# Experts ranked by token count and written out as eight fixed widths in a decoder step

## The chip, the cores and the metric

The kernel runs on one core of a Trainium2 chip. The metric is the device time of one execution in microseconds (us); of several runs the median is given. Engines: PE multiplies matrices, VectorE (DVE), ScalarE (ACT) and GpSimd (POOL) do the elementwise work, SyncE (SP) issues most of the transfers.

## What is computed

One inference step of a two-layer decoder on 520 tokens (a prompt of 512 and 8 samples of one token), width 1024. Each layer has four token mixers behind one input and one output projection; then layer 0 has a dense SwiGLU, layer 1 a SwiGLU of eight experts of which each token takes two. All arithmetic is fp32. What matters here is the second:

```
logits = h @ w_router + b_router
top_v, top_i = top_k(logits, 2);  gates = softmax(top_v)
for e in range(8):
    y = y + comb[..., e:e+1] * ((silu(h @ w1[e]) * (h @ w3[e])) @ w2[e])
```

with h of 520 x 1024, w1[e] and w3[e] of 1024 x 1408, w2[e] of 1408 x 1024. There are 1040 (token, expert) pairs; each expert is computed only for its own.

## The kernel before, in words

The program is one function, `trunk_program`, with one block of code per engine; engines meet by semaphores. Adaptive norm weights, the mixers and the dense layer come first, in straight code (their products are in `product`, L747). Then comes layer 1's expert stage, the part that is changed.

**Routing** (DVE L1603 to L1644). From the router's logits DVE takes the two best experts of each token, counts tokens per expert (`countf`, `count`), sums them up in order of expert to each expert's first row (`ebase`, `first`), and computes each pair's row (`place`). ACT has turned h into rows meanwhile. POOL (L690 to L696) scatters the rows to a table in DRAM, h_by_expert, so that an expert's tokens are next to each other: 10 indirect transfers, 4 KB a row.

**The expert loop.** Every engine runs its own loop over the eight experts (`Fori(0, NE)`) and reads the expert's token count from SBUF into a register. Up to 256 tokens it takes the narrow path, above it a wide path for all 520 columns, which these inputs do not use. On the narrow path of PE:

- `narrow_rows` (L981): waits for the expert's rows, which SP has read into `stage` as two tiles of 128 rows (`first_rows`, L474), and transposes both to columns, 8 transposes a tile (L988). DVE (L1660) and ACT (L1308) copy them from PSUM to `hn`.
- `narrow_by_width` (L1071): a chain of If and Else over ten widths, from 128 to 256 columns; the first that holds the expert's tokens runs, each with its own copy of the code of `narrow_products` (L991).
- `narrow_products`: 11 blocks of w1 and w3 (L1006, 16 matmuls each), then 8 blocks of w2 (L1019, 11 matmuls each); ACT applies silu, DVE multiplies, and ACT copies the result to `yn`. An fp32 matmul shows in the trace as two MATMUL records, so an expert has 352 + 176. After each block of w2, `yn` of the block before is transposed back to rows (L1028, two tiles); DVE copies these to `yrow` (L1671). The last block's transposes wait for ACT's copy.

An expert's weights are 12 chunks (eight of w1 and w3 in turn, four of w2) in a ring of six slots. **SP's order** is written out by hand: the first six chunks of expert 0 when layer 1's projection is done (L464 to L466), then the wait for the scatter (`Rout`, L511), the row tiles of expert 0, and then, for each expert: the next expert's rows once this one's are transposed; each chunk's slot refilled when its products are done (L521 to L527); the expert's result written to y_by_expert (`rows_out`, L491). SP too branches on the count and loops.

**After the loop** POOL waits for the last of those writes (L698) and gathers each token's two results (L703); gating, residual and final norm follow in five tiles of rows, and the output is written.

Of the kernel before, what the change touches and what calls it, by code (L numbers as in the profile page):

```python
# [52 lines left out]
WIDTHS = [128, 136, 144, 152, 160, 176, 192, 208, 224, NW]  # L53
# [46 lines left out]
def trunk_program(nc, A, O):  # L100
    ctx = ExitStack()
    with ctx:
# [87 lines left out]
        ebase = sb("ebase", [P, NE])  # L190
        valid = sb("valid", [P, NT])
# [4 lines left out]
        countf = sb("countf", [P, NE])  # L196
        count = sb("count", [P, NE], I32)
        first = sb("first", [P, NE], I32)
# [98 lines left out]
        def norm_step(tag, k, n):  # L297
# [8 lines left out]
                                          "ya", "ss", "ssr", "rr", "scaled", "mods", "const"]}  # L306
# [16 lines left out]
        def tokens_of(eng, e):  # L323

            return eng.value_load(count[0:1, bass.ds(e, 1)], min_val=0, max_val=T)

        def first_of(eng, e):

            return eng.value_load(first[0:1, bass.ds(e, 1)], min_val=0, max_val=PICKS)
# [8 lines left out]
        def expert_chunk(e, j):  # L338

            if j < 8:  # L340
                w = A["w1_moe" if j % 2 == 0 else "w3_moe"][0]
                n = P * min(3, ET - 3 * (j // 2))
                return w[e].rearrange("(k p) n -> p k n", p=P)[:, :, (j // 2) * 384:(j // 2) * 384 + n], KD, n
            return A["w2_moe"][0][e].rearrange("(k p) n -> p k n", p=P)[:, :, (j - 8) * 256:(j - 7) * 256], ET, 256
# [47 lines left out]
        def _(sp):  # L392
# [71 lines left out]
            sp.wait_ge(*step(1, "po_done", KD))  # L464
            for j in range(EXPERT_RING):
                eload(j, expert_chunk(0, j))  # L466

            def used(e, j):

                if j < 8:  # L470
                    return R["f_done"], ET * e + min(3 * (j // 2) + 3, ET)
                return R["y_done"], KD * e + 2 * (j - 8) + 2

            def first_rows(row):  # L474

                for t in range(2):
                    sp.dma_start(stage[:, t, :], Hd[bass.ds(row + P * t, P), :]).then_inc(Rin[t], 16)

            def rest_of_rows(e):
                c, row = tokens_of(sp, e), first_of(sp, e)  # L480
                with sp.If(c <= NW):
                    for t in range(2, NT):
                        sp.sem_inc(Rwide[t - 2], 16)
                with sp.Else():
                    for t in range(2, NT):
                        free = sp.snap(sp.to_reg(NT * e + t - 1))
                        sp.wait_ge(const_ready, 1)
                        sp.wait_ge(R["in_tr"], free)
                        sp.dma_start(stage[:, t % 2, :], Hd[bass.ds(row + AT[t], P), :]).then_inc(Rwide[t - 2], 16)

            def rows_out(e):  # L491


                c, row = tokens_of(sp, e), first_of(sp, e)
                with sp.If(c <= NW):
                    sp.sem_inc(R["y_out"], 16 * (NT - 2))
                    for t in range(2):
                        there = sp.snap(sp.to_reg(NT * e + NT + t))
                        sp.wait_ge(const_ready, 1)
                        sp.wait_ge(R["yt_ev"], there)  # L500
                        sp.dma_start(Yd[bass.ds(row + P * t, P), :], yrow[:, t, :]).then_inc(R["y_out"], 16)
                with sp.Else():
                    for t in range(NT):
                        there = sp.snap(sp.to_reg(NT * e + t + 2))
                        sp.wait_ge(const_ready, 1)
                        sp.wait_ge(R["yt_ev"], there)
                        sp.dma_start(Yd[bass.ds(row + AT[t], P), :], stage[:, 2, :]).then_inc(R["y_out"], 16)

            sp.wait_ge(R["count"], 2)
            row0 = first_of(sp, 0)  # L510
# [3 lines left out]
            with sp.Fori(0, NE - 1) as e:  # L514
                rest_of_rows(e)
                row = first_of(sp, e + 1)
                free = sp.snap(sp.to_reg(NT * e + NT))
                sp.wait_ge(const_ready, 1)
                sp.wait_ge(R["in_tr"], free)
                first_rows(row)  # L520
                for j in range(PER_E):  # L521
                    which, n = used(e, j)
                    n = sp.snap(sp.to_reg(n))
                    sp.wait_ge(const_ready, 1)
                    sp.wait_ge(which, n)
                    j += EXPERT_RING
                    eload(j, expert_chunk(e, j) if j < PER_E else expert_chunk(e + 1, j - PER_E))  # L527
                rows_out(e)
            last = sp.snap(sp.to_reg(NE - 1))
            rest_of_rows(last)  # L530
            for j in range(PER_E - EXPERT_RING):
                sp.wait_ge(*used(NE - 1, j))
                eload(j + EXPERT_RING, expert_chunk(NE - 1, j + EXPERT_RING))
            rows_out(last)
# [18 lines left out]
        def _(pool):  # L553
# [23 lines left out]
            pool.memset(ebase[:], 0.0).then_inc(R["const"], 1)  # L577
# [120 lines left out]
            pool.wait_ge(R["y_out"], 16 * NE * NT + 16)  # L698
# [17 lines left out]
        def _(pe):  # L716
# [264 lines left out]
            def narrow_rows(e):  # L981

                pe.sem_inc(R["in_tr"], 1)
                for t in range(2):
                    pe.wait_ge(Rin[t], 16 * e + 16)
# [5 lines left out]
            def narrow_products(e, n):  # L991

                for f in range(ET):
                    c = f // 3
                    if f % 3 == 0:
                        chunk_here(e, 2 * c)
                        chunk_here(e, 2 * c + 1)
                    pe.wait_ge(R["f_free"], ET * e + f + 1)
                    m = P * min(3, ET - 3 * c)
                    for w in range(2):  # L1000
                        for k in range(KD):
                            if f == w == 0 and k == 0:
                                pe.wait_ge(R["in_ev"], NT * e + NT)
                            if f == w == 0 and k == 4:
                                pe.wait_ge(R["in_ev1"], 2 * e + 2)
# [3 lines left out]
                pe.wait_ge(R["yt_ev"], NT * e + 1)  # L1009
                pe.sem_inc(R["yt_tr"], 3)  # L1010
                for q in range(KD + 1):
                    if q < KD:
                        if q % 2 == 0:
                            chunk_here(e, 8 + q // 2)
                        pe.wait_ge(R["y_free"], KD * e + q + 1)
                        for k in range(ET):
                            if q == 0 and k in (0, ET - 1):
                                pe.wait_ge(R["f_free"], ET * e + (ET + 1 if k == 0 else ET + 2))
                            mm = pe.matmul(PP[2][:, q % 2, 0:n], expert_slot(8 + q // 2, ET, 256)[:, k, P * (q % 2):P * (q % 2) + P],  # L1019
                                           Gn[:, k, 0:n], start=(k == 0), stop=(k == ET - 1))  # L1020
                        mm.then_inc(R["y_done"], 1)
                    if q:
                        j = q - 1
                        pe.wait_ge(R["y_free"], KD * e + j + 3)
                        if j == 4:
                            pe.wait_ge(R["yt_ev"], NT * e + 4)
                        for t in range(2):
                            tr = pe.transpose(PP[3][:, t, (j % 4) * P:(j % 4) * P + P], yn[:, j, P * t:P * t + P], ident[:])  # L1028
                        if j % 4 == 3:
                            tr.then_inc(R["yt_tr"], 1)  # L1030
# [40 lines left out]
            def narrow_by_width(e, c, widths):  # L1071

                if len(widths) == 1:
                    narrow_products(e, widths[0])
                    return
                with pe.If(c <= widths[0]):
                    narrow_products(e, widths[0])
                with pe.Else():
                    narrow_by_width(e, c, widths[1:])

            pe.wait_ge(R["count"], 2)
            with pe.Fori(0, NE) as e:
                c = tokens_of(pe, e)
                with pe.If(c <= NW):
                    narrow_rows(e)
                    narrow_by_width(e, c, WIDTHS)
                with pe.Else():
                    wide(e)

            pe.wait_ge(R["f_free"], ET * NE + 2)  # L1090
# [8 lines left out]
            pe.wait_ge(R["y_free"], KD * NE + 2)  # L1099
            pe.wait_ge(R["yt_ev"], NT * NE + 1)  # L1100
# [636 lines left out]
```

## Time and profile before

| what | value |
|---|---|
| median of 3 runs | 1824.57 us (1823.91 to 1828.57) |
| span of the profiled execution | 1826.2 us |
| PE busy, share of the span | 1479.6 us, 81% |
| DVE, ACT, POOL busy | 602.4, 480.2, 397.8 us |
| chain that ended last | PE 66%, DVE 15%, issue 9%, DMA 5% |
| all transfers | 286.02 MB, mean 157 GB/s |

The span is what the profile shows of one execution, from its first to its last instruction; it is the profiled execution's own time, and no other is given for it. It lies 1.6 us above the median. "Busy" counts instructions in an engine, not waits; the chain is followed back from the last instruction, at each step to what released it, and "issue" in it is time in which an engine waited for nothing that the profile shows.

### The profile page before, as it was taken

What the parts mean: (1) busy time and instruction counts of PE and PEld (TensorE: products, weight loads), DVE (VectorE), ACT (ScalarE), POOL (GpSimd) and SP (SyncE); (2) the same over time, 40 slices, a digit from 0 to 9 for tenths busy, and PEclk for the clock granted to TensorE, in tenths of its full rate; (3) what the DMA queues carried; (4) which work ended last, traced back from release to release, by engine and by line L of the source; (5) the groups of instructions that cost most, each with busy time, mean ns of one, the idle gap of its engine ahead of it and who ended that gap; (6) DMA issues with size and microseconds to landing.
All of it is one profiled execution on the core that took longest, in us unless ns stands there. A gap on an engine that the chain in (4) does not pass through costs nothing.

```text
span 1826.2 us, 27269 instructions
## 1 busy us (share of the span) xinstructions
PE 1479.6 (81%) x11320; PEld 1411.8 (77%) x11321; DVE 602.4 (33%) x815; ACT 480.2 (26%) x662; POOL 397.8 (22%) x288
## 2 busy tenths in 40 slices
PE   5776877789999999989588859879796919949792
PEld 4555876679999999979577649869796919949692
DVE  6667697623112011146965320101101000000115
ACT  6677312422221122223133221111111100011114
POOL 1102560534434343434524020000000000000004
PEclk9998898899999999989899979889898959979896
DMA  9999121024333322322210469686685833637554
GB/s 321 300 337 316 48 91 46 28 70 120 93 87 98 105 93 56 96 93 70 69 47 6 164 218 306 209 295 210 241 269 183 300 109 110 216 104 234 173 171 163
DMA packets 249862, 286.02 MB, mean 157 GB/s; under 512 B 7589, under 2 KB 241719, under 8 KB 249686
## 3 DMA queue, kind: packets, MB, share of 16 engines
q1 hardware_dynamic: 244886, 272.17, 45.9%
q0 software_dynamic: 3632, 11.08, 1.8%
q8 instruction: 126, 2.06, 0.5%
q10 hardware_dynamic: 1200, 0.56, 0.1%
q14 instruction: 18, 0.15, 0.0%
HBM read 266.45 MB, written 18.05 MB: 156 GB/s over the span
## 4 chain that ended last, share of the span: by engine, by line
PE 66%; DVE 15%; issue 9%; DMA 5%; SPq 2%; ACT 1%; POOL 1%; POOLq 0%; ACTq 0%; DVEq 0%
PE PP L747 28%; PE PP L1006 20%; PE PP L1019 10%; DVE work L1477 7%; DMA mem<-in_w_ada 4%; PE PP L760 2%; DVE stat L1573 1%; PE PP L988 1%; PE PP L792 1%; PE PP L721 1%; PE PP L732 1%; SPq L424 1%; PE PP L1028 1%; DVE stat L1406 1%; DVE mem L1419 1%
## 5 line engine op out<-in xcount | busy, mean ns | idle before, releaser
L747 PE MATMUL PP<-hT_r,mem_r 128*128 128x260 f32 x2624 | 428.5, 284 | 4.6 <-DVE xT L1431 3.2
L1006 PE MATMUL PP<-big,mem 128*128 128x128 f32 (+4 forms) x2816 | 362.4, 293 | 49.5 <-issue 49.2
L1006 PEld LDWEIGHTS PP<-big,mem 128*128 128x128 f32 x2816 | 360.6, 195 | 52.1 <-issue 49.6
L604 POOL TENSOR_TENSOR mem_r<-mem,mem_r 128x1024 fp32r<-128x1024 f32 (+1 forms) x108 | 279.0, 2597 | 407.5 <-ACT mem_r L1132 406.9
L747 PEld LDWEIGHTS PP<-hT_r,mem_r 128*128 128x128 f32 x2624 | 362.4, 188 | 6.4 <-issue 2.5
L747 PE MATMUL PP<-mem_r 128*128 128x260 f32 x1312 | 263.8, 283 | 0.0
L747 PEld LDWEIGHTS PP<-mem_r 128*128 128x128 f32 x1312 | 201.7, 188 | 0.0
L1019 PE MATMUL PP<-big,mem 128*128 128x128 f32 (+4 forms) x1408 | 184.2, 288 | 0.0
L1019 PEld LDWEIGHTS PP<-big,mem 128*128 128x128 f32 x1408 | 178.1, 191 | 0.0
L703 POOL DMA_INDIRECT mem<-y_by_expert,place x10 | 9.6, 956 | 720.7 <-DMA y_by_expert<-work 717.9
L1666 DVE TENSOR_TENSOR big<-PP,big 128x256 f32<-128x256 f32 x88 | 37.4, 425 | 381.3 <-ACT big L1313 381.3
L1132 ACT ACTIVATE mem_r<-mem 128x1024 fp32r<-128x1024 f32 (+1 forms) x108 | 115.9, 1099 | 118.3 <-DMA mem<-in_w_dense 71.0
L747 PE MATMUL PP<-big_r,mem_r 128*128 128x260 f32 x1056 | 129.4, 284 | 2.9 <-DVE big L1592 2.9
L747 PEld LDWEIGHTS PP<-big_r,mem_r 128*128 128x128 f32 x1056 | 127.7, 188 | 3.6 <-DVE big L1592 3.3
L1313 ACT ACTIVATE big<-PP 128x256 f32<-128x256 f32 x88 | 33.8, 384 | 365.8 <-PE PP L1006 365.8
L1477 DVE SCALAR_TENSOR_TENSOR work<-big,vec,work 128x512 f32<-128x512 f32 x120 | 127.1, 1135 | 0.0
L1381 DVE TENSOR_TENSOR mem_r<-mem,mem_r 128x2048 fp32r<-128x2048 f32 x48 | 110.0, 2292 | 45.5 <-ACT mem_r L1148 45.5
L792 PE MATMUL PP<-mem_r,cs_r 128*18 128x256 f32 x768 | 103.6, 295 | 19.3 <-DVE mem_r L1381 18.4
L792 PEld LDWEIGHTS PP<-mem_r,cs_r 128*18 128x18 f32 x768 | 76.9, 102 | 43.7 <-DVE mem_r L1381 23.4
L988 PE MATMUL PP<-ident,stage 128*128 128x128 f32 x128 | 27.0, 399 | 96.6 <-issue 75.4
L988 PEld LDWEIGHTS PP<-ident,stage 128*128 128x128 f32 x128 | 24.3, 214 | 98.6 <-issue 77.0
L1148 ACT ACTIVATE mem_r<-mem 128x2048 fp32r<-128x2048 f32 x48 | 91.7, 1911 | 25.1 <-DMA mem<-in_w_ada 24.9
(239 smaller groups left out, 1155.1 us busy)
## 6 DMA issues: line engine op xcount, KB each, us to landing
mem<-in_w_moe SPq DMA_DIRECT2D x48, 1536.0 KB, 9.8
mem<-in_w_ada SPq DMA_DIRECT2D x48, 1024.0 KB, 11.2
mem<-in_w_moe SPq DMA_DIRECT2D x32, 1408.0 KB, 8.8
mem<-in_w_dense SPq DMA_DIRECT2D x20, 1024.0 KB, 5.6
mem<-in_w_in SPq DMA_DIRECT2D x16, 1024.0 KB, 5.5
mem<-in_w_moe SPq DMA_DIRECT2D x16, 1024.0 KB, 7.0
mem<-in_w_dense SPq DMA_DIRECT2D x16, 704.0 KB, 4.9
mem<-in_w_out SPq DMA_DIRECT2D x8, 1024.0 KB, 5.1
```

The source lines that it names most:

```text
L604: pool.tensor_tensor(r_(raw), raw, read_(hi), ALU.subtract).then_inc(w_lo, 1)
L747: mm = pe.matmul(PP[q][:, h, 0:HT], r_(w[:, k, :]), r_(x[:, k, HT * h:HT * h + HT]), start=(i == 0 and w is wh and x is hi), stop=(i == le ...
L760: mm = pe.matmul(PP[q + c][:, h, 0:HT], r_(w[:, k, :]), r_(x[:, k, HT * h:HT * h + HT]), start=(i == 0 and w is wh and x is hi), stop=(i = ...
L792: mm = pe.matmul(PP[0][0:2 * NQ, j % 2, 0:256], r_(cs[:, k, :]), r_(w[:, k, :]), start=(k == 0 and not lower), stop=(k == KD - 1 and bool( ...
L988: tr = pe.transpose(PP[t][:, h, (j % 4) * P:(j % 4) * P + P], stage[:, t, j * P:(j + 1) * P], ident[:])
L1006: mm = pe.matmul(PP[w][:, f % 2, 0:n], expert_slot(2 * c + w, KD, m)[:, k, P * (f % 3):P * (f % 3) + P], hn[:, k, 0:n], start=(k == 0), st ...
L1019: mm = pe.matmul(PP[2][:, q % 2, 0:n], expert_slot(8 + q // 2, ET, 256)[:, k, P * (q % 2):P * (q % 2) + P], Gn[:, k, 0:n], start=(k == 0), ...
L1132: act.activation(r_(hi), raw, ACT.Copy).then_inc(w_hi, 1)
L1148: act.activation(r_(ahi[:, j % 3]), ada_slot(j), ACT.Copy).then_inc(ada_hi, 1)
L1381: dve.tensor_tensor(r_(ada_slot(j)), ada_slot(j), read_(ahi[:, j % 3]), ALU.subtract).then_inc(ada_lo, 1)
L1477: dve.scalar_tensor_tensor(acc, gin[:, ct, k:k + SEQ], tap("conv_c_w", k, ct), acc, ALU.mult, ALU.add).then_inc(s["conv_tap"], 1)
L1666: dve.tensor_tensor(Gn[:, f, :], PP[1][:, f % 2, 0:NW], hactn[:, f % 2, :], ALU.mult).then_inc(R["f_free"], 1)
```

## The change

Experts are ranked by token count on the device, most first (ties by number), and the eight ranks are written out as straight code of fixed widths. If an expert has more tokens than its rank's width, a flag sends all eight to the wide path, which keeps its loop.

- DVE compares all pairs of experts to get each one's rank and first row, then, after `place`, sorts expert number, first row and count by rank and sets the flag (`over`).
- SP reads the flag and the first rank's expert, and only then loads the first six chunks. Row tiles and row writes come in ones or twos by rank. A result is written after the third chunk of the next rank.
- PE has no loop or branch on the way. `rows_in` of the next rank stands after the sixth block of w2, and the last block's way back (`row_of_y`) after the first block of the next rank.
- ACT and DVE copy only the rank's width.
- SP waits for the last row write and signals `all_out`, for which POOL now waits.

The core of the diff (the wide path, which only changes its loop's place, is left out):

```diff
-WIDTHS = [128, 136, 144, 152, 160, 176, 192, 208, 224, NW]
+RANK_WIDTH = [208, 160, 152, 144, 136, 136, 128, 128]
+RANK_TILES = [-(-n // P) for n in RANK_WIDTH]
...
+        def expert_at(eng, r):
+            return eng.value_load(rank_i[0:1, 1, bass.ds(r, 1)], min_val=0, max_val=NE - 1)
+        def first_at(eng, r):
+            return eng.value_load(rank_i[0:1, 2, bass.ds(r, 1)], min_val=0, max_val=PICKS)
+        def tiles_before(r):
+            return sum(RANK_TILES[:r])
...
             sp.wait_ge(*step(1, "po_done", KD))
+            sp.wait_ge(R["count"], 1)
+            flag = over_of(sp)
+            expert0 = expert_at(sp, 0)
             for j in range(EXPERT_RING):
-                eload(j, expert_chunk(0, j))
+                eload(j, expert_chunk(expert0, j))
+            row0 = first_at(sp, 0)
             for t in range(NT):
                 sp.wait_ge(Rout[t], 32)
             first_rows(row0)
-            with sp.Fori(0, NE - 1) as e:
...
+            with sp.If(flag <= 0):
+                row = row0
+                expert = expert0
+                for r in range(NE):
+                    if r + 1 < NE:
+                        next_row = first_at(sp, r + 1)
+                        next_expert = expert_at(sp, r + 1)
+                        sp.wait_ge(R["in_tr"], 2 * tiles_before(r + 1))
+                        first_rows(next_row, r + 1)
+                    for j in range(PER_E):
+                        if r + 1 == NE and j + EXPERT_RING >= PER_E:
+                            break
+                        sp.wait_ge(*used(r, j))
+                        g = j + EXPERT_RING
+                        eload(g, expert_chunk(expert, g) if g < PER_E else expert_chunk(next_expert, g - PER_E))
+                        if r and j == 2:
+                            rows_out(r - 1, before_row)
+                    before_row, row, expert = row, next_row, next_expert
+                rows_out(NE - 1, row)
+                sp.wait_ge(R["y_out"], 16 * tiles_before(NE))
+            with sp.Else():
...
+            sp.sem_inc(R["all_out"], 1)
...
-            pool.wait_ge(R["y_out"], 16 * NE * NT + 16)
+            pool.wait_ge(R["all_out"], 1)
...
+            def rows_in(r):
+                for t in range(RANK_TILES[r]):
+                    pe.wait_ge(Rin[t], 16 * (r + 1 if t == 0 else second_tiles(r + 1)))
                     for h in range(2):
                         for j in range(4 * h, 4 * h + 4):
                             tr = pe.transpose(PP[t][:, h, (j % 4) * P:(j % 4) * P + P], stage[:, t, j * P:(j + 1) * P], ident[:])
                         tr.then_inc(R["in_tr"], 1)
...
+            def row_of_y(r, j):
+                base, n = 2 * tiles_before(r), RANK_TILES[r]
+                pe.wait_ge(R["y_free"], KD * r + j + 1)
+                if j % 4 == 0 and (r or j):
+                    pe.wait_ge(R["yt_ev"], base + (n if j else 0))
+                for t in range(n):
+                    tr = pe.transpose(PP[3][:, t, (j % 4) * P:(j % 4) * P + P], yn[:, j, P * t:P * t + P], ident[:])
+                if j % 4 == 3:
+                    tr.then_inc(R["yt_tr"], 1)
...
+            def narrow(r):
+                n = RANK_WIDTH[r]
                 for f in range(ET):
...
                     mm.then_inc(R["f_done"], 1)
+                    if r and f == 0:
+                        row_of_y(r - 1, KD - 1)
+                for q in range(KD):
...
+                    mm.then_inc(R["y_done"], 1)
                     if q:
+                        row_of_y(r, q - 1)
+                    if q == 5 and r + 1 < NE:
+                        rows_in(r + 1)
...
-            with pe.Fori(0, NE) as e:
-                c = tokens_of(pe, e)
-                with pe.If(c <= NW):
-                    narrow_rows(e)
-                    narrow_by_width(e, c, WIDTHS)
...
+            flag = over_of(pe)
+            with pe.If(flag <= 0):
+                rows_in(0)
+                for r in range(NE):
+                    narrow(r)
+                row_of_y(NE - 1, KD - 1)
...
-            dve.tensor_copy(count[:], countf[:]).then_inc(R["count"], 1)
-            for e in range(1, NE):
-                link(dve.tensor_tensor(ebase[:, e:e + 1], ebase[:, e - 1:e], countf[:, e - 1:e], ALU.add))
-            dve.tensor_copy(first[:], ebase[:]).then_inc(R["count"], 1)
+            link(dve.scalar_tensor_tensor(key[:], countf, float(NE), eidx[:], ALU.mult, ALU.subtract))
+            link(dve.tensor_tensor(above[:], key[:].unsqueeze(1).to_broadcast([P, NE, NE]),
+                                   key[:].unsqueeze(2).to_broadcast([P, NE, NE]), ALU.is_gt))
+            link(dve.tensor_tensor(above_n[:], above[:], countf.unsqueeze(1).to_broadcast([P, NE, NE]), ALU.mult))
+            dve.tensor_reduce(rank[:], above[:], AX.X, ALU.add)
+            link(dve.tensor_reduce(firstf, above_n[:], AX.X, ALU.add))
...
             dve.tensor_copy(place[:], placef[:]).then_inc(R["route"], 1)
 
+            link(dve.tensor_tensor(at_rank[:], rank[:].unsqueeze(1).to_broadcast([P, NE, NE]),
+                                   eidx[:].unsqueeze(2).to_broadcast([P, NE, NE]), ALU.is_equal))
+            link(dve.tensor_tensor(by_rank[:], at_rank[:].unsqueeze(1).to_broadcast([P, 3, NE, NE]),
+                                   of_expert[:].unsqueeze(2).to_broadcast([P, 3, NE, NE]), ALU.mult))
+            link(dve.tensor_reduce(of_rank[:], by_rank[:], AX.X, ALU.add))
+            dve.tensor_copy(rank_i[:], of_rank[:])
+            link(dve.tensor_tensor(overf[:], of_rank[:, 0, :], room[:], ALU.is_gt))
+            link(dve.tensor_reduce(over_maxf[:], overf[:], AX.X, ALU.max))
+            link(dve.tensor_copy(over[:], over_maxf[:]))
+            dve.sem_inc(R["count"], 1)
```

## Rows read from the trace of the kernel before

**Rows 1.** The chain of waits from 980 us to the end: shares by line.

```profile
by line: PE PP L1006 42.8%; PE PP L1019 20.7%; issue 16.4%; PE PP L747 4.1%; PE PP L988 3.0%; PE PP L1028 1.7%; PE PP L949 1.1%; DVE mem L1700 0.9%; POOL h_by_expert L695 0.9%; PE PP L732 0.9%; DMA mem<-y_by_expert,place 0.6%; DVE mem L1701
```

**Rows 2.** The same chain, pieces in order of time: start us, us, what.

```profile
1079.88 39.61 PE PP L1006 x352
...
1124.41 0.22 PE PP L1028 x2
...
1479.47 26.30 issue
...
1782.69 0.45 PE PP L1028 x2
```

**Rows 3.** PE by form, 1076 to 1784 us: busy, mean | idle before, releaser.

```profile
L1006 PE MATMUL PP<-big,mem 128*128 128x128 f32 x1056 | 118.9, 275 | 0.3 <-DVE big L1660 0.3
L1006 PE MATMUL PP<-big,mem 128*128 128x136 f32 x704 | 84.9, 285 | 0.5 <-issue 0.5
L1006 PE MATMUL PP<-big,mem 128*128 128x208 f32 x352 | 64.3, 347 | 26.3 <-issue 26.3
L1019 PE MATMUL PP<-big,mem 128*128 128x128 f32 x528 | 62.4, 275 | 0.0
L1006 PE MATMUL PP<-big,mem 128*128 128x152 f32 x352 | 48.0, 301 | 12.0 <-issue 12.0
L1006 PE MATMUL PP<-big,mem 128*128 128x144 f32 x352 | 46.3, 298 | 10.4 <-issue 10.4
L988 PE MATMUL PP<-ident,stage 128*128 128x128 f32 x128 | 27.0, 399 | 96.6 <-issue 75.4 <-DMA stage<-h_by_expert 21.3
```

**Rows 4.** Branches L1076, L1082 on PE's sequencer: ns min/median/max, first and last start.

```profile
L1076 PEldq COMPARE_BRANCH  x30: 64/3898/6695, 1077.5 to 1782.7; - x30
...
L1082 PEldq COMPARE_BRANCH  x8: 67/7231/7511, 1147.8 to 1783.0; - x8
```

**Rows 5.** L1006 alone: us, PE and PEld busy (x), clock, DMA share, GB/s.

```profile
1085.00:1119.49 34.49, 34.49 (x309) 34.30 (x308) 1.00 0.63 201
...
1158.00:1190.00 32.00, 32.00 (x278) 32.00 (x278) 1.00 0.52 163
...
1309.54:1320.00 10.46, 10.46 (x61) 10.46 (x62) 0.71 0.01 2
1320.00:1350.00 30.00, 30.00 (x247) 30.00 (x247) 1.00 0.54 172
...
1515.00:1565.00 50.00, 50.00 (x287) 50.00 (x286) 1.00 0.42 132
...
1640.00:1675.00 35.00, 35.00 (x274) 35.00 (x273) 1.00 0.52 161
```

**Rows 6.** All engines: us, busy by engine (x), clock, DMA share, GB/s.

```profile
1060.00:1070.00 10.00, 0.00 (x0) 0.00 (x0) 0.00 (x0) 0.00 (x0) 7.56 (x9) 0.50 0.95 373
1120.00:1140.00 20.00, 20.00 (x182) 20.00 (x181) 1.66 (x3) 2.69 (x7) 0.00 (x0) 1.00 1.07 371
```

**Rows 7.** The start of the stage in order of time: start us, us, what.

```profile
1028.41 15.75 SPq L399 DMA_DIRECT2D mem<-in_w_moe  x6
...
1055.37 0.77 DVE L1633 TENSOR_TENSOR totals<-totals 128x8 f32<-128x8 f32 x4
...
1058.13 1.09 POOL L695 DMA_INDIRECT h_by_expert<-work,place  x1 [20.83 <-DVE place L1639]
...
1069.53 3.17 DMA h_by_expert<-stage,place
...
1076.21 3.67 PE L988 MATMUL PP<-ident,stage 128*128 128x128 f32 x16 [21.26 <-DMA stage<-h_by_expert]
```

**Rows 8.** The page, costliest groups: products of the mixer and dense stages.

```profile
L747 PE MATMUL PP<-hT_r,mem_r 128*128 128x260 f32 x2624 | 428.5, 284 | 4.6 <-DVE xT L1431 3.2
```

**Rows 9.** SP's register loads (L325); row writes (L501) from issue to landing.

```profile
L325 SPq TENSOR_LOAD <-count x16: 268/286/1438, 1074.1 to 1755.4; - x16
...
DMA to landing us min/median/max: 2.7/7.2/9.3
```

More of the change, by code:

```diff
@@ L321, in expert_slot, with over_of, second_tiles @@
             return cut(mem, (j % EXPERT_RING) * EXPERT_SLOT, k, cols)
[L323 to L329, printed above, removed]
+        def over_of(eng):
+            return eng.value_load(over[0:1, 0:1], min_val=0, max_val=1)
+        def expert_at(eng, r):
[4 more added lines that the diff above has]
+            return sum(RANK_TILES[:r])
+        def second_tiles(r):
+            return sum(n > 1 for n in RANK_TILES[:r])
         w_in_v = [A["w_in"][l].rearrange("(k p) (b n) -> b p k n", p=P, n=256) for l in range(DEPTH)]
@@ L462, in _, with used, first_rows, rest_of_rows @@
                     mixer_loads(1)
+            def used(r, j):
+                if j < 8:
+                    return R["f_done"], ET * r + min(3 * (j // 2) + 3, ET)
+                return R["y_done"], KD * r + 2 * (j - 8) + 2
+            def first_rows(row, r=None):
+                for t in range(2 if r is None else RANK_TILES[r]):
+                    sp.dma_start(stage[:, t, :], Hd[bass.ds(row + P * t, P), :]).then_inc(Rin[t], 16)
+            def rest_of_rows(r):
+                row = first_at(sp, r)
+                for t in range(2, NT):
+                    free = sp.snap(sp.to_reg(NT * r + t - 1))
+                    sp.wait_ge(const_ready, 1)
+                    sp.wait_ge(R["in_tr"], free)
+                    sp.dma_start(stage[:, t % 2, :], Hd[bass.ds(row + AT[t], P), :]).then_inc(Rwide[t - 2], 16)
@@ L479, in rest_of_rows @@
[L479 to L507, printed above, removed]
@@ new lines, in _ @@
+            with sp.Else():
+                with sp.Fori(0, NE - 1) as r:
+                    rest_of_rows(r)
+                    row = first_at(sp, r + 1)
+                    free = sp.snap(sp.to_reg(NT * r + NT))
+                    sp.wait_ge(const_ready, 1)
+                    sp.wait_ge(R["in_tr"], free)
+                    first_rows(row)
+                    this, then = expert_at(sp, r), expert_at(sp, r + 1)
+                    for j in range(PER_E):
+                        which, n = used(r, j)
+                        n = sp.snap(sp.to_reg(n))
+                        sp.wait_ge(const_ready, 1)
+                        sp.wait_ge(which, n)
+                        j += EXPERT_RING
+                        eload(j, expert_chunk(this, j) if j < PER_E else expert_chunk(then, j - PER_E))
+                    wide_rows_out(r)
+                end = sp.snap(sp.to_reg(NE - 1))
+                rest_of_rows(end)
+                last = expert_at(sp, NE - 1)
+                for j in range(PER_E - EXPERT_RING):
+                    sp.wait_ge(*used(NE - 1, j))
+                    eload(j + EXPERT_RING, expert_chunk(last, j + EXPERT_RING))
+                wide_rows_out(end)
+                sp.wait_ge(R["y_out"], 16 * NE * NT + 16)
@@ L1069, in wide @@
                     tr.then_inc(R["yt_tr"], 1)
[L1071 to L1081, printed above, removed]
[L1082 to L1090 removed]
+            pe.wait_ge(R["count"], 1)
+            flag = over_of(pe)
+            with pe.If(flag <= 0):
+                rows_in(0)
+                for r in range(NE):
+                    narrow(r)
+                row_of_y(NE - 1, KD - 1)
+                pe.wait_ge(R["f_free"], ET * NE)
+                pe.wait_ge(R["y_free"], KD * NE)
+                pe.wait_ge(R["yt_ev"], 2 * tiles_before(NE))
+            with pe.Else():
+                with pe.Fori(0, NE) as r:
+                    wide(r)
+                pe.wait_ge(R["f_free"], ET * NE + 2)
+                pe.wait_ge(R["y_free"], KD * NE + 2)
+                pe.wait_ge(R["yt_ev"], NT * NE + 1)
             pe.wait_ge(R["diag"], 1)
```

223 lines of the change are left out of this document (110 added, 113 removed).

## The prediction, made before the changed kernel was built or run

> **What bounds the kernel now.** I read the chain of waits of the last half first: in the stretch from 980 us to the end TensorE's expert products (L1006, L1019) hold 63% of the chain, and "issue", time in which an engine waited for nothing that the profile shows, holds 16% [rows 1]. The expert stage runs from the first product at 1079.88 us to the last turned-back tile at 1782.69 + 0.45 = 1783.14 us [rows 2]: 703.3 us, where PE is the chain nearly throughout. Grouped by form, the lines say what fills it [rows 3]: the forms are the branch widths of the eight experts (1056 + 704 records of L1006 are three experts of 128 columns and two of 136, 352 each; one each of 144, 152 and 208), and beside them stand "issue" gaps of 75.4 us before the row transposes (L988) and 26.3, 12.0, 10.4 and 0.5 us before products: 124.6 us. Those gaps belong to branches: the 30 compare-and-branches of the chain of widths (L1076) take 3898 ns in the median and up to 6695, the eight of the loop's end (L1082) 7231 in the median [rows 4]. The expert of 208 columns, which passes seven Else arms, waits 26.30 us in one piece [rows 2]. Last, the clock: after a gap products start at a granted clock of 0.71 (between the two levels of 1.2 and 2.4 GHz), later at 1.00 [rows 5].
>
> Transfers do not bound the stage. The stage's weights are, by their shapes, 8 x 3 x 1024 x 1408 x 4 bytes = 138 MB, 197 GB/s over 703 us; for 20 us on end the queues moved 371 GB/s, and 373 during the scatter [rows 6].
>
> **The change, part by part.** I count the stage anew, since after it the stage is one straight stream on PE.
>
> *Widths.* Time of one record at full clock, from undisturbed stretches [rows 5]: 34.49/309 = 0.1116 us at 128 columns, 32.00/278 = 0.1151 at 136, 0.1215 at 144, 0.1277 at 152, 0.1742 at 208. The fixed width 160 is not in the trace; it lies between 0.1277 and 0.1742, and the slope from 152 to 208 gives 0.1343. Sorted, the old widths are 208, 152, 144, 136, 136, 128, 128, 128; the ranks are 208, 160, 152, 144, 136, 136, 128, 128. Each rank holds its expert, and four are 8 columns wider. An expert has 528 records (352 + 176). Sum: 528 x (0.1742 + 0.1343 + 0.1277 + 0.1215 + 2 x 0.1151 + 2 x 0.1116) = 533.9 us; the widening alone costs about 12 us.
>
> *Transposes.* At speed one takes 0.22/2 = 0.11 us [rows 2], where L988 after a gap takes 3.67/16 = 0.23 [rows 7]. Ranks of 128 move one tile instead of two, so 14 tiles remain; the first rank's two stand before the stream. Rows in: 12 x 8 x 0.11 = 10.6 us; rows back: 14 x 8 x 0.11 = 12.3 us. Set inside products they need no wait: what each waits for (ACT's copy, a DVE copy) has a product of 22 records, 2.5 us or more, to finish in. If that cover failed, each border would again have a wait on a copy as it has now, no more.
>
> *Gaps, loop, branches.* Straight code has no gap to price; the nearest rows are the long straight products of the dense stage, L747, 4.6 us idle over 2624 records, 3.2 of it waiting for VectorE [rows 8], and L1019, which follows 352 records without idle time [rows 3]. I take 0, with a few branch-sized waits of 3.9 us as the upper end. Stage: 533.9 + 10.6 + 12.3 = 556.8 us, against 703.3: **-146.5 us**. Of this 124.6 are gaps; about 15 are the slow starts of L1006 (its five busy times less records times the prices above: 1.0 + 3.9 + 3.0 + 3.0 + 3.5 [rows 3]); the rest is transposes at half speed and border waits, less the 12 of wider ranks.
>
> *Do the weights keep up?* A rank of 128 needs 138/8 = 17.3 MB in 528 x 0.1116 + 1.8 = 61 us, 284 GB/s, below 371 [rows 6]. Six slots hold three pairs, and a pair lasts 96 x 0.1116 = 10.7 us against 3.1 MB/0.371 = 8.5 us of transfer. I expect no wait here.
>
> *The first load is moved, and this costs.* Before, SP issues the six first loads when the projection is done, at 1028.41, and the issues take 15.75 us since the queue takes so much at a time [rows 7]; the transfers then run beside the router. After, SP needs the first rank's expert, so the loads wait for the count, which VectorE now gives after the row places and seven more small operations. Four linked ones take 0.77 us today [rows 7], 0.2 each; with larger tiles I estimate 1.8 us in all. The places are ready about 1 us before the scatter's first work at 1058.13 [rows 7], in either kernel (ranking replaces the seven additions of the old bases), so the count comes near 1058.6, and with two register loads on SP (0.3 us each, 1.4 at most [rows 9]) the first issue near 1060. That is in the middle of POOL's scatter of 1040 rows of 4 KB (4.3 MB), which already moves 373 GB/s by itself [rows 6]. SP's own row reads (L477, 1.05 MB), for which PE waits, are issued behind the six loads on the same queue. Until data flows I count 1.3 us (the least landing of a 512 KB row write, 2.7 us [rows 9], less 1.4 of transfer). At 1061.3 some 3.5 MB of scatter, 9.4 MB of weights and 1.05 MB of rows are left: 13.95 MB/0.373 = 37.4 us, to 1098.7. Then the first rank's transposes, 3.67 us [rows 7], and products from 1102.4 instead of 1079.88: **+22.5 us**. The order on the queue is the choice here. For it: the row writes of the stage, issued while weights are under way, land after 7.2 us in the median, 2.7 at the least [rows 9]. Low end: rows overtake what the queue still holds when the sixth issue returns. Today that is 15.75 us after the first, when 14.4 x 0.373 = 5.4 MB are through; with 3.5 MB of scatter that is 8.9/0.373 = 23.9 us, 1085.2, and 1.05 MB at half the rate take 5.6 more: +14. High end: the mix moves only what the scatter alone did from its first issue at 1058.13 to its last landing at 1069.53 + 3.17 [rows 7], 4.26 MB in 14.6 us = 292 GB/s: +33.
>
> *Tail.* Today POOL waits for the last row write itself. After, SP waits for it, leaves its If and gives POOL the signal; one row tile less is copied and written, which I count at nothing. A branch takes 64 ns on PE at the least and 7511 at the most [rows 4]. SP's wide path, over which it goes, is a loop and a few dozen transfers, against well over a thousand matmuls in PE's, and nothing else is being transferred by then, so I take the low price: +0.1, up to +7.5.
>
> **Sum:** -146.5 + 22.5 + 0.1 = -123.9 us. The profiled execution's span is 1826.2; against the median of the three runs, 1824.6 (1.6 less), the forecast is 1824.6 - 123.9 = 1700.7, say **1701 us**.
>
> The rows put 30 branches at 3898 ns in the median and eight at 7231 [rows 4], and the sum above follows them. A rule speaks against it: the Trainium skill, Advanced Engine Details and Errata (section Control Flow Timing), puts a compare-and-branch at about 108 ns. By that rule 38 branches cost 4 us, the gaps are something else, and the sum would be about -3 us; the measured medians are 36 and 67 times that figure.
>
> **Rivals.**
> (A) The first loads overlap better or worse than I think. That is the range, 1692 (+14) to 1711 (+33).
> (B) *Slower: straight code runs dry.* No block of code is run twice, so if PE waited for code along the stream as it does at branches, 3.9 us each [rows 4], 32 waits, four a rank, would eat the 123.9 us. At six a rank the time is 1701 + 48 x 3.9 = 1888 us. Against it: L747 and L1019, above, run on without idle time [rows 3, 8]. For it: the branch waits show that code arrives late when it is not next in line.
> (C) *The gaps hid a weight limit.* If the queues sustain only the 197 GB/s that they moved on average, the same 138 MB take 703 us and nothing but the start's loss stays: 1824.6 + 22.5 = 1847. Against it: 371 GB/s for 20 us on end [rows 6].
> (D) *The gaps are not the branches'* but belong to whatever a new expert begins with, and return at the borders: -146.5 + 124.6 + 22.5 = +1: about 1825. Against it: the gap grows with the Else arms, 26.30 us at seven [rows 2], 0.5 at one [rows 3]. (This is where the Trainium skill's Control Flow Timing would lead.)
> (E) The change doesn't do what it says: one expert over its rank's width sends all eight to the wide path, 520 columns; at 208 columns' price scaled, 0.1742 x 2.5 x 4224 = 1840 us for the products alone, over a millisecond slower. The forms exclude it for these inputs [rows 3].
> (F) Partial: some border waits stay, 2 to 10 us a rank: 1717 to 1781.
>
> **Numbers.** Forecast with A: 0.82. F beyond the range: 0.12. D: 0.03. B, C and E: 0.01 each. The range takes A, the tail's upper end and about one such wait a rank of 1 us: 1692 - 3 = 1689 (some 1 us for a price of a width read a few tenths of a percent off, and the tile less in the tail) to 1711 + 7.5 + 8 = 1727. A measurement of this kernel tells about 0.3% (5.5 us) from no change. Faster is the forecast with F, 0.94; D is "same", 0.03; B, C and E are slower, 0.03.
>
> **What the changed profile would show.** Right: L1006 and L1019 without "issue" before them; the granted clock at 1.00 from about 1106 us to the end of the stage; six loads issued after 1059 us, and L988's first wait, on the row reads, ending near 1099; the first product near 1102 and the last tile turned near 1660; the stage 557 us long. A queue order that lets rows pass shows as a first product before 1096. Wrong: "issue" before PE records inside ranks (B), waits on weight slots before L1006 (C), gaps of 5 to 13 us at each rank's start (D, F), 260-column forms (E), or a POOL gather that starts over 1 us after the last row landed (tail).

## The result, and the profile after

The changed kernel takes 1715.16 us in the median of four runs, the kernel before 1824.24 beside it: a ratio of 0.9393, 95% interval 0.9379 to 0.9406, 109 us saved. The forecast was 1701, the range 1689 to 1727.

First the chain of waits of the changed kernel, pieces in order of time (start us, us, what), with the lines that answer to [rows 2] and [rows 7]. L1070, L1083, L1036 and L1046 are the old L1006, L1019, L988 and L1028; L427 and L501 are SP's weight and row transfers (old L399 and L477).

```profile
1089.14 12.40 DMA stage<-h_by_expert
1101.59 3.67 PE PP L1036 x16
1105.28 62.95 PE PP L1070 x352
...
1188.46 3.87 PE PP L1083 x22
1192.55 1.75 PE PP L1036 x16
1194.29 3.87 PE PP L1083 x22
1202.47 4.35 PE PP L1070 x32
1206.82 0.22 PE PP L1046 x2
1207.04 43.47 PE PP L1070 x320
...
1666.99 0.34 PE PP L1046
1667.36 0.70 DVE work L1733
1668.08 5.09 DMA y_by_expert<-work
1673.22 2.46 issue
1675.69 0.27 issue
```

The border from the first rank to the second reads off line by line: two blocks of w2 with the next rank's 16 row transposes between them (1192.55, 1.75 us, 0.11 each as forecast), the first block of the next rank (1202.47), the last tile of the old one (1206.82), and on. There is no piece of issue in it. Before, such a border held up to 13 us of issue before the transposes and up to 26 behind them.

PE by form in the stage (busy, mean ns | idle before, releaser), to be held against [rows 3], and two stretches (us, busy and count by engine, granted clock, DMA share, GB/s), against [rows 5, 6]:

```profile
L1070 PE MATMUL PP<-big,mem 128*128 128x208 f32 x352 | 63.0, 342 | 0.0
L1070 PE MATMUL PP<-big,mem 128*128 128x160 f32 x352 | 48.1, 299 | 0.0
L1083 PE MATMUL PP<-big,mem 128*128 128x208 f32 x176 | 32.1, 339 | 0.0
L1036 PE MATMUL PP<-ident,stage 128*128 128x128 f32 x112 | 15.3, 294 | 44.1 <-DMA stage<-h_by_expert 44.1
```
```profile
1110.00:1200.00 90.00, 90.00 (x525) 89.79 (x524) 6.79 (x15) 7.39 (x20) 0.00 (x0) 1.00 0.54 176
1210.00:1660.00 450.00, 450.00 (x3760) 450.00 (x3759) 44.44 (x109) 43.16 (x139) 0.00 (x0) 1.00 0.82 274
```

No product waits for "issue", PE is busy 450 of 450 us at a granted clock of 1.00 (2.4 GHz), and the queues move 274 GB/s at 0.82 of their time: the weights keep up. From one profile to the other, 1826.2 to 1713.8, the 112.4 us divide so:

| stretch | before | after | difference | forecast |
|---|---|---|---|---|
| to the first product | 1079.88 | 1105.28 | +25.4 | +22.5 |
| first product to the last tile turned back | 703.3 | 562.1 | -141.2 | -146.5 |
| from there to the end | 43.1 | 46.5 | +3.4 | +0.1 |

### The profile page after: what moved, and what is told of

The parts are those of the page before. It is cut to its first block, busy times and chain, and to the rows that moved or that the text cites. A ratio compares the mean times of both kernels' runs of the same rounds, so it can differ in the third digit from the quotient of the medians.

```text
span 1713.8 us, 26036 instructions
## 1 busy us (share of the span) xinstructions
PE 1469.0 (86%) x11288; PEld 1405.1 (82%) x11288; DVE 589.3 (34%) x811; ACT 446.3 (26%) x644; POOL 398.9 (23%) x296
## 4 chain that ended last, share of the span: by engine, by line
PE 71%; DVE 16%; DMA 6%; SPq 3%; issue 2%; ACT 2%; POOL 0%; POOLq 0%; ACTq 0%; DVEq 0%
PE PP L796 30%; PE PP L1070 21%; PE PP L1083 10%; DVE work L1537 7%; DMA mem<-in_w_ada 4%; PE PP L809 2%; PE PP L841 2%; DVE stat L1633 2%; SPq L427 1%; PE PP L770 1%; PE PP L781 1%; PE PP L1036 1%; DVE stat L1466 1%; DVE mem L1479 1%; DVE mem_r L1475 1%
## 5 line engine op out<-in xcount | busy, mean ns | idle before, releaser
L796 PE MATMUL PP<-hT_r,mem_r 128*128 128x260 f32 x2624 | 429.7, 284 | 4.6 <-DVE xT L1491 3.2
L1070 PE MATMUL PP<-big,mem 128*128 128x128 f32 (+5 forms) x2816 | 361.8, 291 | 0.0
L1070 PEld LDWEIGHTS PP<-big,mem 128*128 128x128 f32 x2816 | 360.0, 191 | 0.4 <-issue 0.4
L1083 PE MATMUL PP<-big,mem 128*128 128x128 f32 (+5 forms) x1408 | 187.9, 291 | 0.0
L1083 PEld LDWEIGHTS PP<-big,mem 128*128 128x128 f32 x1408 | 182.0, 191 | 0.0
L1739 DVE TENSOR_TENSOR big<-PP,big 128x136 f32<-128x136 f32 (+5 forms) x88 | 27.6, 313 | 371.9 <-ACT big L1370 371.9
L1370 ACT ACTIVATE big<-PP 128x136 f32<-128x136 f32 (+5 forms) x88 | 26.0, 295 | 334.8 <-PE PP L1070 334.8
L1202 ACT ACTIVATE mem_r<-mem 128x2048 fp32r<-128x2048 f32 x48 | 91.7, 1911 | 24.3 <-DMA mem<-in_w_ada 24.2
L1652 DVE TENSOR_TENSOR big<-PP,work 128x520 f32<-128x520 f32 x22 | 15.4, 700 | 221.6 <-ACT work L1330 221.6
L809 PE MATMUL PP<-hT_r,mem_r 128*128 128x260 f32 x320 | 58.3, 301 | 29.4 <-POOL mem_r L667 25.8
```

What stands on the lines that cost most here:

```text
L796: mm = pe.matmul(PP[q][:, h, 0:HT], r_(w[:, k, :]), r_(x[:, k, HT * h:HT * h + HT]), start=(i == 0 and w is wh and x is hi), stop=(i == le ...
L809: mm = pe.matmul(PP[q + c][:, h, 0:HT], r_(w[:, k, :]), r_(x[:, k, HT * h:HT * h + HT]), start=(i == 0 and w is wh and x is hi), stop=(i = ...
L1070: mm = pe.matmul(PP[w][:, f % 2, 0:n], expert_slot(2 * c + w, KD, m)[:, k, P * (f % 3):P * (f % 3) + P], hn[:, k, 0:n], start=(k == 0), st ...
L1202: act.activation(r_(ahi[:, j % 3]), ada_slot(j), ACT.Copy).then_inc(ada_hi, 1)
L1739: dve.tensor_tensor(Gn[:, f, 0:n], PP[1][:, f % 2, 0:n], hactn[:, f % 2, 0:n], ALU.mult).then_inc(R["f_free"], 1)
```

## The experiments

Differences are taken against the changed kernel's 1715.2 us; run again, it took 1715.9 (the last run below).

**Jumps put back.** Theory: a jump to code that is not next in line makes PE wait. First with a whole rank's code to jump over, then with a few instructions.

```diff
                 for r in range(NE):
-                    narrow(r)
+                    with pe.If(flag <= 0):
+                        narrow(r)
+                    with pe.Else():
+                        narrow(r)
```

The second run has `pe.wait_ge(const_ready, 1)` in the Else instead.

> Each rank's products on PE are put into an If whose Else holds a second, never used copy of the same code, so that PE jumps over one rank's worth of code eight times. Theory (a jump to code that is not next in line makes PE's sequencer wait, 3.9 to 7.2 us by the branch lines of the kernel before, of which the work already queued on PE may hide up to about 3.5 us): 10 to 45 us slower than the changed kernel, 1725 to 1760, with gaps marked issue at each rank's end and a granted clock under 1.00 after them. Rival (a compare-and-branch itself is cheap, the gaps of before belonged to what a new expert begins with): within 2 us of the changed kernel.

> The same eight Ifs on PE, but each Else holds one satisfied wait, so the jump goes a few instructions on. Theory (the distance costs, not the branch): within 2 us of the changed kernel, 1715. Rival (each branch costs its 4 to 7 us wherever it goes): as slow as the run with far jumps.

Measured: 1750.95 us with far jumps, 35.8 more; 1714.12 with near ones, 1.0 less. The added branches on PE's sequencer (ns min/median/max): far, the two of them at the border from the first to the second rank in that run, and near.

```profile
L1135 PEldq COMPARE_BRANCH  x16: 73/1677/6333, 1101.5 to 1695.8; - x16
L1135 PEldq COMPARE_BRANCH  x2: 82/1714/3345, 1197.4 to 1200.8; - x2
```
```profile
L1135 PEldq COMPARE_BRANCH  x16: 64/120/312, 1101.9 to 1663.0; - x16
```

The sixteen are of two kinds, so no branch took the median: eight tests at a rank's start, which go straight on (73 to 82 ns in the far run, 64 to 70 in the near one), and eight jumps over the Else at a rank's end, 3272 to 6333 ns when far and 169 to 312 when near. The pages of the two runs also count the packets of the queue that the profile calls instruction (packets, MB, share), far and near:

```profile
q8 instruction: 102, 1.67, 0.4%
```
```profile
q8 instruction: 86, 1.41, 0.3%
```

Then the chain of the run with far jumps at the same border, with PE, its clock and DMA in one stretch of each of the two (columns as above):

```profile
1200.54 0.48 issue
1201.02 0.65 PE PP L1070 x3
1201.66 2.57 issue
1204.23 7.02 PE PP L1070 x29
```
```profile
1200.00:1210.00 10.00, 6.95 (x29) 6.60 (x28) 0.00 (x0) 0.34 (x1) 0.00 (x0) 0.67 0.77 265
```
```profile
1200.00:1210.00 10.00, 10.00 (x75) 9.97 (x74) 1.52 (x3) 0.83 (x3) 0.00 (x0) 1.00 0.76 262
```

The same eight jumps cost nothing when they go a few instructions on and 4.5 us each when they go over a rank. From the first product to the last tile the stage lasts 595.6 us with far jumps and 561.4 with near ones; of the 34 us some 24 are issue, and some 9 are products that run slower behind it. At the border shown, the jump starts at 1197.4, while PE still works off what is queued, and takes 3.35 us, of which 0.48 come out as issue. The second piece, 2.57 us after three records, stands on no branch's row. Behind it the clock is down (0.67 over that stretch, 1.00 with near jumps).

The instruction queue moved 16 packets more with far jumps than with near ones or in the changed kernel (86), two of 16 KB for each jump; from 1195 to 1206 us it moved two with far jumps and none with near ones. So code is fetched at these jumps, and PE stands still meanwhile.

The Trainium skill, Advanced Engine Details and Errata (Control Flow Timing), gives 108 ns for a compare-and-branch; the near run's 64 to 312 are of that size, the far jumps' 3272 to 6333 and the 7231 of [rows 4] are not. The Trainium skill, Runtime: NRT & Kernel Launch (Instruction fetch mechanics), says that a taken branch to code outside the current window waits until that code is fetched; the two more packets for each far jump agree.

**The first loads.** Theory: the row reads stand behind six loads on SP's queue. One run issues only two loads ahead of the rows, the other all six before the count, with the heaviest expert's number written in (the first six loads then do not follow the ranking).

```diff
-            for j in range(EXPERT_RING):
+            for j in range(2):
                 eload(j, expert_chunk(expert0, j))
             row0 = first_at(sp, 0)
             for t in range(NT):
                 sp.wait_ge(Rout[t], 32)
             first_rows(row0)
+            for j in range(2, EXPERT_RING):
+                eload(j, expert_chunk(expert0, j))
```
```diff
+            for j in range(EXPERT_RING):
+                eload(j, expert_chunk(5, j))
             sp.wait_ge(R["count"], 1)
             flag = over_of(sp)
             expert0 = expert_at(sp, 0)
-            for j in range(EXPERT_RING):
-                eload(j, expert_chunk(expert0, j))
```

> SP issues two of the six first loads, then waits for the scatter and reads the rows, then issues the other four. Theory (SP's queue is served in order, so the row reads wait for the six loads ahead of them, and the start costs 23 us): rows land after some 7.4 MB instead of 13.9 MB from 1064 us on, near 1085 instead of 1101.6; the second pair of weights lands before PE needs it; about 16 us faster than the changed kernel, 1699 (1696 to 1703). Rival (rows pass the loads on the queue, and the start is late because of the count or the shared bandwidth): no faster than 1712.

> The six first loads are issued before the count is known, as in the kernel before, for the expert that heads the ranking with these inputs, written in as a number (left out: that the first six loads follow the ranking). Theory (the moved loads are the whole cost of the later start): first product near 1082.5 us, 23 us faster than the changed kernel, 1692 (1689 to 1695). Rival (the later start is VectorE's longer ranking or SP's registers): under 5 us faster.

Measured: 1698.46 us (16.7 less) and 1690.98 (24.2 less). SP's issues in order of time, the changed kernel, then the two runs:

```profile
1063.14 25.12 SPq L427 DMA_DIRECT2D mem<-in_w_moe  x6
1089.14 3.82 SPq L501 DMA_DIRECT2D stage<-h_by_expert  x2
```
```profile
1062.08 1.85 SPq L427 DMA_DIRECT2D mem<-in_w_moe  x2
1080.80 0.91 SPq L501 DMA_DIRECT2D stage<-h_by_expert  x2
1081.89 9.60 SPq L427 DMA_DIRECT2D mem<-in_w_moe  x4
```
```profile
1030.05 15.79 SPq L427 DMA_DIRECT2D mem<-in_w_moe  x6
1074.29 8.39 SPq L501 DMA_DIRECT2D stage<-h_by_expert  x4
```

In the changed kernel six issues take 25.12 us, against 15.79 where no scatter runs beside them; that fits a queue which takes loads only as fast as they move (369 GB/s from 1064 to 1089 us). The row reads go out at 1089.14 and land 12.40 later, behind what is still queued. Behind two loads they go out at 1080.80 and have landed at 1086.7; with the loads done early they go out at 1074.29, near the 1072.94 of before the change. Both results lie within a microsecond or so of the theory: the changed kernel's later start is nearly all the six loads and their place in the queue, not the ranking on VectorE.

**The placement alone.** Each rank's transposes are put back to its own borders.

```diff
                 for r in range(NE):
+                    rows_in(r)
                     narrow(r)
-                row_of_y(NE - 1, KD - 1)
+                    row_of_y(r, KD - 1)
...
-                    if r and f == 0:
-                        row_of_y(r - 1, KD - 1)
...
-                    if q == 5 and r + 1 < NE:
-                        rows_in(r + 1)
```

(ACT's and DVE's copies move with them.)

> The placement alone is undone: each rank transposes its own rows before its first product, and its last block back to rows before it ends; ranks, widths and straight code stay. Theory (placed, the borders cost nothing but the transposes themselves; unplaced, PE waits at each of seven borders for ACT's copy of the last block, about 0.4 us, and for the copies of the new rows, about 0.8 us): 7 to 11 us slower than the changed kernel, 1723 (1721 to 1727), granted clock still 1.00 in the stage, no issue gaps. Rival (the placement is what removed the gaps): over 40 us slower.

Measured: 1725.42 us, 10 more. One border in the chain of this run:

```profile
1276.12 0.31 ACT work L1369
1276.48 0.45 PE PP L1046 x2
1276.95 1.29 DVE work L1727 x2
1278.24 1.20 DVE big L1721 x2
1279.58 15.48 PE PP L1070 x118
```

From ACT's copy of the last block at 1276.12 to the next product at 1279.58 are 3.46 us. Some 2 of them are transposes that are needed anyway (0.22 and 1.75, as in the changed kernel's border above); the rest, about 1.5, are the wait for ACT and what VectorE's copies last beyond the transposes. The old rank's two (1.29) stand ahead of the new rank's (1.20) there. Seven times 1.5 is the 10 us. The clock stays at 1.00 from 1110 to 1640 us, and no product waits for issue: the rival fell. So the placement is worth 10 us, and the gaps of before stay away without it.

**The signal.** It is given inside each branch, behind the wait for the last row write.

```diff
                 sp.wait_ge(R["y_out"], 16 * tiles_before(NE))
+                sp.sem_inc(R["all_out"], 1)
...
                 sp.wait_ge(R["y_out"], 16 * NE * NT + 16)
-            sp.sem_inc(R["all_out"], 1)
+                sp.sem_inc(R["all_out"], 1)
```

> SP gives POOL its signal inside each branch, behind the last wait, instead of after the join. Theory (the 2.46 us of issue between SP's If and its signal are the jump over the wide path): the piece disappears and the kernel is 2 to 3 us faster than the changed one, 1712.5. Rival (the time is the landing of the row write or POOL's start): no piece disappears, within 1 us.

Measured: 1713.39 us (1710.89 to 1714.35), 2 less. The chain after the last row write:

```profile
1666.42 5.10 DMA y_by_expert<-work
1671.54 0.02 SPq L555
1671.56 0.27 issue
```

The 2.46 us piece at 1673.22 of the changed kernel is gone, and the landing is unchanged (5.10). The time alone, with its spread of 3.5 us, would not show so small a gain; the chain does.

**The widths.** The ranks get the widths that these inputs need.

```diff
-RANK_WIDTH = [208, 160, 152, 144, 136, 136, 128, 128]
+RANK_WIDTH = [208, 152, 144, 136, 136, 128, 128, 128]
```

> Rank widths 208, 152, 144, 136, 136, 128, 128, 128: the widths that the kernel before chose for these experts, sorted. Theory (records cost 0.1359, 0.1293, 0.1227, 0.1159 and 0.1118 us at 160, 152, 144, 136 and 128 columns in the changed kernel's stage, 528 to a rank, so the widening costs 12.7 us, and one tile less saves 16 transposes of 0.11): 14.5 us faster than the changed kernel, 1701 (1699 to 1703). Rival (the weights' transfers bound the stage once the gaps are gone): PE waits for weights and the gain is under 5 us.

Measured: 1700.12 us, 15 less. PE by form in its stage:

```profile
L1070 PE MATMUL PP<-big,mem 128*128 128x128 f32 x1056 | 118.8, 275 | 0.0
L1083 PE MATMUL PP<-big,mem 128*128 128x128 f32 x528 | 61.5, 275 | 0.0
```

1056 + 528 records of 128 columns, none idle: with three ranks at the width that asks most of the queues, PE still waits for no weights.

**Together.** Two loads ahead of the rows, the signal inside, narrower ranks.

> Two loads ahead of the rows, the signal inside the branch and the narrower ranks together. Theory (they lie in different stretches of one chain): the gains add up, 16.7 + 14.5 + 2.5 = 34 us faster than the changed kernel, 1681.5 (1679 to 1685). Rival (with narrow ranks the ring of weights, begun four loads late, becomes the wait): over 1690, with waits on weight slots in the first two ranks.

Measured: 1680.86 us (1679.54 to 1683.05), 0.9199 of the kernel before (0.9182 to 0.9215), 34 to 35 less than the changed kernel. The parts add up, as expected of different stretches of one chain, and the rival fell: in its profile no group of products has idle time ahead of it. It beats both kernels. Its widths are those that these inputs need; a heavier draw would fall back on the wide path earlier.

**The kernel before with one width, and the changed one again.**

```diff
-WIDTHS = [128, 136, 144, 152, 160, 176, 192, 208, 224, NW]
+WIDTHS = [208]
```

> The kernel before with one width, 208 columns, for all eight experts: its loop stays, its chain of If and Else goes. Theory (the gaps before the products are the chain's jumps, those before the row transposes the loop's and the paths'): of 49.2 us of issue before L1006 under 2 are left, before L988 40 to 80 us stay; products take 528 x 8 x 0.1759 = 743 us instead of some 526, so with 49 us of gaps and about 10 of slow clock gone the time is near 1985 (1965 to 2000). Rival (a gap belongs to each new expert, whatever the branches): issue before L1006 stays near 49 and the time is over 2025.

> The changed kernel itself, unchanged, beside the kernel before in the same call: 1715 (1713 to 1717), and a spread of its runs of under 4 us, where the kernel before, with its jumps, spreads over 8 us and more.

Measured: 1922.66 us with one width; the changed kernel again 1715.94 (1714.28 to 1716.21), the kernel before beside it 1821.74 to 1829.53. In the run with one width, the loop's branch and, by form, what stood before the products and the row transposes (columns as in [rows 3, 4]), then the issue at two of its borders:

```profile
L1082 PEldq COMPARE_BRANCH  x8: 67/209/254, 1180.6 to 1875.2; - x8
```
```profile
L1006 PE MATMUL PP<-big,mem 128*128 128x208 f32 x2816 | 497.4, 339 | 2.1 <-DVE big L1660 2.1
L988 PE MATMUL PP<-ident,stage 128*128 128x128 f32 x128 | 19.1, 313 | 36.3 <-DMA stage<-h_by_expert 21.4 <-issue 14.8
```
```profile
1175.65 6.94 issue
1182.60 3.67 PE PP L988 x16
...
1281.56 1.32 issue
```

The chain's gaps before L1006 are gone, as expected. The second half of the expectation was wrong: I had given the gaps before L988 to the loop and the paths, and of 75.4 us only 14.8 stayed, 6.94 of them at the first turn and about 1.3 at each later one. These 60.6 us account for the miss, 62 us below the expected 1985.

Two jumps make up a gap before L988 in the kernel before: the one out of the chain, from the end of the copy that ran past all the code behind it (L1076), then the loop's (L1082). Here they are at the border behind the second expert, where PE idles for 13.18 us (the 64 ns are the next expert's first test):

```profile
L1076 PEldq COMPARE_BRANCH  x2: 64/2424/4783, 1217.2 to 1230.9; - x2
L1082 PEldq COMPARE_BRANCH  x1: 7404/7404/7404, 1222.2 to 1222.2; - x1
```

Over the seven borders the jumps out of the chain take 31 us and the loop's 37. With one width both kinds of jump are still there, and they are cheap from the second turn on: the one past the wide path (L1084) took 5252 ns at the first turn and at most 182 later, the loop's 209 in the median. So the loop is not dear in itself. Nor does distance alone make its jump dear: in the kernel before the same jump took 248 and 220 ns behind the first and the third expert, which run the first copy (128 columns), and 7.2 to 7.5 us behind the other five.

```profile
L1084 PEldq COMPARE_BRANCH  x16: 76/126/5252, 1058.5 to 1874.9; - x16
```

After the first turn of the run with one width, from 1185 to 1880 us, the instruction queue (q8) moved nothing; in the kernel before it moved 69 packets from 1185 to 1784. So what a jump costs goes with whether its code has to be fetched again: with ten copies mostly yes, with one no. How much code stays at hand, no run here shows.

## Why the prediction was right, and where it was off

The direction, the mechanism and the range held; the likeliest time was 14.5 us too low (1715.2 against 1700.7).

*Gaps.* Right: all 124.6 us are gone, and jumps that are put back bring gaps back, 4.5 us a jump. Rival B (straight code runs dry) fell: 450 us on end without idle time. Rival D fell with the near jumps. What I had not seen is how the sum splits: 49 us, before products, are the chain's tests; the 75 before the row transposes are mostly the jumps out of the chain (31) and the loop's (37), of which some 60 us go when one copy stands in place of ten.

*Clock.* Right: 1.00 through the stage but for the first few records, which run slower after the long wait for rows (62.95 us for 352 records of 208 columns, where 352 x 3.87/22 would be 61.9; about 1 us not counted).

*Widths.* The step that failed by most: the price of a record was read off stretches by dividing their length by the count beside it. That count holds records that only reach into the stretch, so the prices came out 0.2 to 1.3% low: 0.1742 at 208 columns where the chain has 3.87/22 = 0.1759. With the chain's 0.1759, 0.1359, 0.1293, 0.1227, 0.1159 and 0.1118 the eight ranks take 538.1 us instead of 533.9: 4.2 of the error. The interpolated price of 160 columns was 0.1343, measured 0.1359. The run with narrower ranks confirms the size of the widening, 15 us with the tile it saves.

*Transposes.* Right: 0.11 us each, no wait at the borders. Unplaced they cost 10.

*Weights.* Right; rival C fell: no product waits for a slot, with 274 GB/s over 450 us.

*The first load.* Right in kind and size. Rows landed at 1101.54 against 1098.7 forecast, but the places were ready 2.2 us later than in the profile of before (VectorE's L1701 at 1059.19, old L1639 at 1057.03), although the ranking is shorter than the additions that it replaces. These 2.2 us arise in stages that the change does not touch; their cause was not looked for. From there on the start cost 0.7 us more than forecast. The choice of the queue's order, which spanned +14 to +33, was the right one: four loads fewer ahead of the rows gave 16.7 us back.

*Tail.* Wrong by 3.3 us. The jump over SP's wide path cost 2.46 us, not 0.1; the low price was taken because SP's path holds less code than PE's and nothing else is transferred by then, and that was no reason. The row write, one tile less, took 0.9 us longer from VectorE's last copy to its landing (5.1 against 4.2 us); why is open.

*The base.* I had set the median 1.6 us below the span of the profiled execution. In every execution for which both are on record, the time is 1.8 us above the span (1715.62 against 1713.8 here). So the profiled execution of before, with its span of 1826.2, took some 1828.0 us (an estimate), 3.8 above the median of 1824.24, and a sum made in it was set against a median that is not its own. After, the median is 1.4 above the span. The 1.6 and the 1.4 are 3.0 us of the error. With the prices of the widths, the slow first records, the late places, the rest of the start and the tail, 4.2 + 1.0 + 2.2 + 0.7 + 3.3 + 3.0 = 14.4 of the 14.5.

## What to carry to other kernels

Code that is chosen by branches from many large copies costs more than the branches: here jumps between the copies, and most jumps of the loop around them, waited microseconds for code. Written out in the order of execution the same work ran without gaps, and in a loop with one copy it had one gap of 7 us and then about 1.3 us a turn. When a load is made to wait for a decision, look at what stands behind it on its queue: here PE waited for the small row reads behind the weights, and issuing fewer loads ahead of them gave back two thirds of the loss.

## What had not been expected

- A jump's wait is only in part on the branch's own row. PE's far jumps show 3272 to 6333 ns there, the beginning hidden by queued work, and at three borders a second piece of issue follows 3 to 43 records into the next rank. SP's branch over the wide path (L535) shows 38 ns at the most, and the 2.46 us stand behind it as issue.
- Whether a loop's jump is dear depends on what was run in between: with ten copies 7.2 to 7.5 us mostly, but 220 to 248 ns where the first copy had run; 209 ns in the median with one copy.
- Far jumps go with a wide spread of the runs: 6.8 us over four runs with them (1747.58 to 1754.4), 6 to 10 in the kernel before, 0.9 to 3.5 in all other runs. That the jumps cause the spread is not shown.
